# Differential attention run inside and between the tiles of the input projection

## The reference, cut to what matters

```
proj = rms_norm(x, norm_mix_g) @ w_in             # 1024 -> 1952
q_d, k_d, v_d, c_q, c_kv, k_pe = split(proj)      # 512, 512, 512, 256, 128, 32
# differential attention, 8 heads of 2 x 32, values 64 wide, causal, distance bias
a = softmax(q1 k1' * s + bias) - lam * softmax(q2 k2' * s + bias)
o = a @ v;  o = o * rsqrt(mean(o*o) + eps) * out_gain * (1 - lambda_init)
# latent attention, 8 heads
q = rms_norm(c_q)  @ w_uq      # 256 -> 8 x 96, the last 32 of each head rotated
kv = rms_norm(c_kv) @ w_ukv    # 128 -> 8 x (64 key + 64 value)
key = [kv's key, rotated k_pe (shared by the heads)];  o2 = softmax(q key' * s, causal) @ v
x = x + concat(o, rms_norm(o2)) @ w_out           # then memory attention, experts, second block
```

## Time and profile before

| | |
|---|---|
| runs, median (lowest to highest) | 2230.72 us (2230.46 to 2231.52) |
| the profiled execution, its own time | 2235.1 us |
| its span, first to last instruction | 2233.3 us |
| TensorE / VectorE / ScalarE / GpSimd busy | 2000.9 / 1089.9 / 793.4 / 118.6 us |
| mean granted TensorE clock | 0.926 of 2.4 GHz |
| bytes moved by DMA | 261.07 MB, mean 117 GB/s |

### The profile page before, as it was taken

How to read it: one execution, slowest core, us unless ns; L and a number is a source line. 1 busy time by engine, 2 the same in 40 slices (tenths; PEclk the granted TensorE clock), 3 DMA queues, 4 the chain that set the end, 5 groups by cost and what they waited for, 6 DMA issues and landing times.

```text
span 2233.3 us, 25577 instructions
## 1 busy us (share of the span) xinstructions
PE 2000.9 (90%) x9978; PEld 1544.0 (69%) x9978; DVE 1089.9 (49%) x1998; ACT 793.4 (36%) x1655; POOL 118.6 (5%) x85
## 2 busy tenths in 40 slices
PE   7988777897897776999897999999998999999997
PEld 6733444776564445878797888888876768888886
DVE  5565454635321113768555544554465655434444
ACT  4154454444121113653355332222341643322232
POOL 0000000000100003402132000000000000000000
PEclk9966887998899897999998999999998989999999
DMA  5100230334799996121100223233221012322321
GB/s 190 35 0 1 85 97 19 117 114 148 294 411 411 406 393 231 57 67 67 57 1 5 86 95 103 86 95 97 92 95 57 1 44 90 103 95 88 103 94 46
DMA packets 78391, 261.07 MB, mean 117 GB/s; under 512 B 9376, under 2 KB 11680, under 8 KB 77888
## 3 DMA queue, kind: packets, MB, share of 16 engines
q1 hardware_dynamic: 68112, 231.47, 29.1%
q0 software_dynamic: 5040, 19.58, 2.8%
q10 hardware_dynamic: 5120, 8.39, 1.0%
HBM read 242.62 MB, written 16.79 MB: 116 GB/s over the span
## 4 chain that ended last, share of the span: by engine, by line
PE 76%; DVE 10%; DMA 8%; ACT 4%; issue 2%; POOL 0%; ACTq 0%; SPq 0%; DVEq 0%; POOLq 0%
PE ps_pair L276 18%; PE ps_pair L278 17%; PE ps_pair L277 17%; DMA split_acts_as_f<-w_experts 6%; PE ps_pair L794 5%; PE ps_pair L1649 3%; PE ps_turn L807 2%; PE ps_turn L2157 2%; PE ps_out L821 2%; PE ps_shared L821 2%; PE ps_pair L2157 1%; DVE ps_pair L897 1%; PE ps_shared L1660 1%; DMA w_raw<-w_gdnin 1%; PE ps_shared L496 1%
## 5 line engine op out<-in xcount | busy, mean ns | idle before, releaser
L276 PE MATMUL ps_pair<-split_acts,w_high 128*128 128x512 f32 (+1 forms) x1824 | 718.5, 394 | 26.8 <-DVE split_acts L572 9.9
L277 PE MATMUL ps_pair<-split_acts,w_high 128*128 128x512 f32 (+1 forms) x1824 | 710.3, 389 | 0.0
L278 PE MATMUL ps_pair<-split_acts,w_low 128*128 128x512 f32 (+1 forms) x1824 | 710.2, 389 | 0.0
L237 DVE TENSOR_TENSOR w_low<-w_raw,w_high 128x1024 fp32r<-128x1024 f32 (+5 forms) x257 | 291.9, 1136 | 283.5 <-ACT w_high L231 281.6
L276 PEld LDWEIGHTS ps_pair<-split_acts,w_high 128*128 128x128 f32 x1824 | 347.0, 190 | 107.5 <-issue 22.9
L278 PEld LDWEIGHTS ps_pair<-split_acts,w_low 128*128 128x128 f32 x1824 | 346.4, 190 | 72.2
L277 PEld LDWEIGHTS ps_pair<-split_acts,w_high 128*128 128x128 f32 x1824 | 347.1, 190 | 68.8 <-issue 0.2
L231 ACT ACTIVATE w_high<-w_raw 128x1024 fp32r<-128x1024 f32 (+5 forms) x257 | 251.0, 978 | 228.4 <-PE ps_pair L278 203.7
L1649 PE MATMUL ps_pair<-split_acts_as_f 128*64 128x256 f32 x512 | 130.1, 412 | 39.6 <-DMA split_acts_as_f<-w_experts 33.4
L1651 PE MATMUL ps_pair<-split_acts_as_f 128*64 128x256 f32 x512 | 130.6, 413 | 0.0
L1649 PEld LDWEIGHTS ps_pair<-split_acts_as_f 128*64 128x64 f32 x512 | 73.5, 149 | 76.2 <-issue 48.1
(11 more groups left out here) (460 smaller groups left out, 2260.7 us busy)
## 6 DMA issues: line engine op xcount, KB each, us to landing
split_acts_as_f<-w_experts SPq DMA_DIRECT2D x192, 512.0 KB, 14.0
w_raw<-w_gu SPq DMA_DIRECT2D x88, 512.0 KB, 3.4
w_raw<-w_down SPq DMA_DIRECT2D x32, 448.0 KB, 3.3
w_raw<-w_gdnin SPq DMA_DIRECT2D x26, 512.0 KB, 3.4
w_raw<-w_out SPq DMA_DIRECT2D x24, 512.0 KB, 3.5
rows_y<-scratch ACTq DMA_DIRECT2D x64, 128.0 KB, 6.2
w_raw<-w_down SPq DMA_DIRECT2D x16, 512.0 KB, 3.4
w_raw<-w_in SPq DMA_DIRECT2D x15, 512.0 KB, 4.3
```

Source lines behind the costliest of these rows:

```text
L237: dve.tensor_tensor(WL[:, t % SPLIT, 0:kt * m], WRAW[:, t % RING, 0:kt * m], WH[:, t % SPLIT, 0:kt * m].bitcast(F32), ALU.subtract).then_i ...
L276: pe.matmul(out, wh[:, k, :], self.high(k), start=(k == 0), stop=False)
L277: pe.matmul(out, wh[:, k, :], self.low(k), start=False, stop=False)
L278: last = pe.matmul(out, wl[:, k, :], self.high(k), start=False, stop=(k == self.kt - 1))
```

## The change

The input projection's tiles come in another order: c_q and c_kv first (tiles 12, 13, 14), then for each pair of heads its query, key and value tile. Differential attention is cut into calls of `gap(n)`, each of which issues on TensorE the scores of group n, the turning of group n-2 and the values of group n-3, on ScalarE the copies of n-2 and n-3 and then the exponentials of n, on VectorE the weights of n-1 and then the extreme of n. It has one bank pair of its own, `pairs[1]`, and one bank for its outputs. Gaps 0 to 21 stand in the middle of and behind each of tiles 5 to 14 and of `kpe`, gaps 22 to 29 behind every second tile of `uq` and `ukv`, 30 to 32 after them, 33 and 34 at the opening of latent attention. The waits between scores, extremes and exponentials are now for each member of a group (in all five kinds of attention a score matmul and an exponential each signal).

The norms of c_q and c_kv stand behind tiles 1 to 4, the angles behind tiles 1 and 4, the distances behind tile 0. Each rotation is a step of its own (`single`), behind tiles of `uq` and `ukv`, as are the turning of each head's values and the copy of the shared key. The head norm, its split and the first three squares of the latent norm stand behind groups of latent attention. The places in memory change to suit. GpSimd's load of the memory tokens waits for `ukv` too, the load of the router for latent attention's end.

```
+IN_ORDER = (12, 13, 14, 0, 4, 8, 1, 5, 9, 2, 6, 10, 3, 7, 11)
...
+            def gap(self, n):
+                here = lambda k: 0 <= k < len(self.groups)
+                if here(n - 2):
+                    self.number(n - 2)
+                def tensor(pe):
+                    if here(n):
+                        if n % PER_PAIR == 0:
+                            self.wait_scores(pe, n // PER_PAIR)
+                        self.pe_scores(pe, n)
+                    if here(n - 2):
+                        self.pe_turn(pe, n - 2)
+                    if here(n - 3):
+                        self.pe_values(pe, n - 3)
+                def scalar(act):
+                    if here(n - 2):
+                        self.act_turn(act, n - 2)
+                    if here(n - 3):
+                        self.act_out(act, n - 3)
+                    if here(n):
+                        self.act_exp(act, n)
+                def vector(dve):
+                    if here(n - 1):
+                        self.dve_probs(dve, n - 1)
+                    if here(n):
+                        self.dve_max(dve, n)
...
             def pe_scores(self, pe, n):
-                if n >= len(self.banks):
-                    need(pe, "att_act", ("exp", m - len(self.banks)))
-                elif m >= 2:
-                    need(pe, "att_act", ("exp", m - 2))
+                before = m - (len(self.banks) if n >= len(self.banks) else 2)
                 for j, (h, i, r) in enumerate(members):
+                    if before >= 0:
+                        need(pe, "att_act", ("exp", before, sizes[before] - 1 if n < len(self.banks) else j | 1 if len(members) > 2 else j))
...
+            def single(self, k):
...
+                def tensor(pe):
+                    self.waits(pe, k)
+                    claim(pe)
+                    done(pe.matmul(ps_m[r, :], self.perm[r, r], x, start=True, stop=True), "rope_pe", (self.name, k))
+                    held.append(("rope_dve", (self.name, "swap", k)))
+                def vector(dve):
...
+                    done(dve.tensor_tensor(SC[r, k % 2, :], ps_m[r, :], self.sin[r, :], ALU.mult), "rope_dve",
+                         (self.name, "swap", k))
+                    done(dve.tensor_tensor(x, x, self.cos[r, :], ALU.mult), "rope_dve", (self.name, "cos", k))
+                    self.join(dve, k)
...
+        diff.banks = pairs[1:]
...
+        beside = defaultdict(list, {0: [early], 1: [n_cq.part(0), n_cq.part(1), angles_m.part(0)],
+                                    2: [n_cq.root(), n_ckv.part(0)], 3: [n_cq.spread(), n_ckv.root()],
+                                    4: [n_ckv.spread(), angles_m.part(1), early_exps]})
+        first = at_in[8]
+        places = [side[j] for j in range(first, 15) for side in (middle, beside)] + [k_middle[0], k_beside[0]]
+        for n, here in enumerate(places):
+            here.append(diff.gap(n))
+            c, off = divmod(n, 6)
+            if c < QT and off == 3:
+                here.append(turn_values(c))
...
+        for j, rope, gap in ((1, 0, 1), (2, 1, 0), (3, 2, 1), (4, 3, 0), (5, 4, 1), (6, 5, 0), (7, None, 1)):
...
+        for j, rope, head, gap in ((0, 6, None, 0), (1, None, 0, 1), (2, 7, 1, 0), (3, None, 2, 1), (4, 8, 3, 0),
+                                   (5, None, 4, 1), (6, None, 5, 0), (7, None, 6, 1)):
...
+        fl += [diff.gap(n), values_and_keys(7)]
...
+        mla.opened = [diff.gap(n + 1)]
...
+        at_group = [[head_norm.square(0)], [head_norm.sum(0), head_norm.square(1)],
+                    [head_norm.sum(1), head_norm.square(2)], [head_norm.sum(2), head_norm.square(3)],
+                    [head_norm.sum(3), n_mo.part(0)], [head_norm.roots()], [head_norm.spread(0)],
+                    [head_norm.spread(1), s_diff.one(0)], [head_norm.spread(2), s_diff.one(1), n_mo.part(1)],
+                    [head_norm.spread(3), s_diff.one(2)], [s_diff.one(3)], [], [n_mo.part(2)], [], []]
+        for k, stages in enumerate(at_group):
+            mla.beside[k + 1] += stages
+        fl += [mla, n_mo.part(3), n_mo.root(), n_mo.spread()]
...
             need(pool, "rope_dve", ("mla_q", MLA_HEADS))
+            wait_products(pool, "ukv")
             done(pool.dma_start(raw1, a["mem_t"]), "ld_mem", by=16)
```

More of the change, by code:

```diff
@@ L716, in __init__ @@
                 self.m0, self.h0, self.o0 = seen_groups["n"], seen_heads["n"], seen_outs["n"]
[L717 to L720, removed]
+                self.u0, self.opened = [0] * len(self.groups), []
+                if not lazy:
+                    for n in range(len(self.groups)):
+                        self.number(n)
+                sizes.extend(len(group[0]) for group in self.groups)
                 seen_groups["n"] += len(self.groups)
@@ L774, in tensor @@
                 self.pe_scores(pe, 1)
+                for stage in self.opened:
+                    stage.tensor(pe)
                 for n in range(len(self.groups)):
@@ L780, in tensor @@
                         self.pe_values(pe, n - 1)
+                    for stage in self.beside.get(n, ()):
+                        stage.tensor(pe)
                 self.pe_values(pe, len(self.groups) - 1)
@@ L833, in scalar @@
                         self.act_out(act, n - 1)
+                    for stage in self.beside.get(n, ()):
+                        stage.scalar(act)
                 self.act_out(act, len(self.groups) - 1)
@@ L878, in vector @@
                     self.dve_probs(dve, n)
+                    for stage in self.beside.get(n, ()):
+                        stage.vector(dve)
             def dve_max(self, dve, n):
@@ new lines, in program, with values_and_keys, scalar @@
+        rope_q = Rope("mla_q", [ROPED[0:96]] + [AF[0:96, 8 + h, :] for h in range(MLA_HEADS)], 96,
+                      const("perm_mla"), cos_m, sin_m, rope_waits)
+        def values_and_keys(h):
+            turn = Transposes(f"mla_v{h}", [
+                ([(keys_at[h][:, i * P:(i + 1) * P], i * P) for i in range(QT)],
+                 (G[:, 12:16, h * 64:(h + 1) * 64],
+                  lambda b: b[:, :].rearrange("p (i c) -> p i c", c=P)[:, :, 64:128]), None)],
+                wait_first=lambda e: (wait_evac(e, BASE["ukv"] + h), need(e, "mla_dve", "kpe")))
+            mla_v.append(turn.t0)
+            def scalar(act):
+                turn.scalar(act)
+                need(act, "rope_dve", ("mla_q", 0))
+                done(act.copy(keys_at[h][64:96], ROPED[64:96]), "mla_act", "keys")
+            return On(tensor=turn.tensor, scalar=scalar)
@@ L1246, in diff_gain @@
+        mla.opened = [diff.gap(n + 1)]
+        for k in range(len(mla.groups)):
+            mla.number(k)
+            mla.beside[k] = []
+        mla.beside[0].append(diff.gap(n + 2))
         def diff_gain(dve, k, s, label):
```

297 lines of the change are left out of this document (196 added, 101 removed).

## The result

| | before | after | forecast |
|---|---|---|---|
| runs, median (lowest to highest) | 2231.12 us (2230.46 to 2232.25) | 2199.36 us (2197.24 to 2205.47) | 2166.0 us |
| the profiled execution, its span | 2233.3 us | 2203.6 us | |
| first matmul of `out` | 373.7 us | 336.45 us | 309.0 us |
| mean granted TensorE clock | 0.926 | 0.933 | |

The change makes the kernel 31.8 us faster, a ratio of 0.9861 (95% interval 0.9848 to 0.9875). The direction is as forecast and the time lies in the wide range (2134 to 2204), not in the forecast's own (2148 to 2184); the gain is half of the 64.7 us that were forecast.

A forecast was written before the change was run, and what follows sets the result against it. Differential attention was taken as TensorE at the lower clock with gaps, inside a serial stretch to 373.70 us. Parts 1 to 4 put `out` at 309.0, 64.7 earlier: 2230.7 - 64.7 = 2166.0 us; own range 2148 to 2184, wide 2134 to 2204.

The forecast's parts named there:

- part 1: Input projection, tiles 0 to 5: gap 1 begins at 74.9 us, not 54.6; +20.3, of which 15.1 TensorE standing still.
- part 2: 21 gaps in tiles 6 to 14 and `kpe`: 9.5 us a tile, `kpe` ends at 172.4 us.
- part 3: `uq`, `ukv`, rotations, values, keys and 8 gaps: 52 us, to 224.4; then gaps 30 to 32: 9 us, to 233.4.
- part 4: Latent attention with the head norm inside: 67.1 us, to 300.5; then 8.5 of remaining norm, `out` starting at 309.0.
- part 5: The rest of the kernel: later loads cost nothing, finer waits and signals 0, between -3 and +4 us.
- The rival of catching orders: Orders of three engines catch everywhere: projection +22, part 3 64 us, part 4 74 us; total 2198; chance 0.19.
- the ring through VectorE and ScalarE: Part 2: scores wait for exponentials, these for extremes; 2.95 us a gap, 9.5 a tile, longer than TensorE's 8.4.
- The rival of the hidden ring: Ring is hidden and TensorE the bound, in parts 1 to 3: 8.4 us a tile, total 2141; chance 0.20.
- the 0.15 us hops: Part 2: a term of 0.15 us for hops within the 2.95 us ring of each gap.
- the third rival: Clock falls in the mixed stretch: 16.8 us a two-gap tile, +77, part 3 +15; total 2258; chance 0.03.

The follow-up runs named there:

- one group later: Changed kernel with each step of head norm, split and latent squares cut by engine, VectorE's part one group after TensorE's, ScalarE's copy after that; 2177.39 us.
- gaps in a row: Changed kernel with gaps 0 to 21 taken out of the input projection's tiles and set in a row behind `kpe`; 2246.42 us.
- both together: Changed kernel with the angles in pieces behind later tiles and the head norm's vector side a group later; 2165.13 us.

## Why the prediction was right or wrong

| step | forecast | measured | miss |
|---|---|---|---|
| part 1: to gap 1 | 74.9 | 78.2 | +3.3 |
| part 2: to the end of `kpe` | 97.5 more, 172.4 | 94.5, 172.7 | -3.0 |
| part 3: `uq`, `ukv` | 52 | 52.6 | +0.6 |
| part 3: gaps 30 to 32 | 9 | 11.9 | +2.9 |
| part 4: latent attention | 67.1 | 95.1 | +28.0 |
| part 4: rest ahead of `out` | 8.5 | 4.1 | -4.4 |
| part 5 | 0 | 5.4 | +5.4 |

**Part 4 is the step that failed:** the 67.1 us of latent attention with the head norm inside took 95.1. The forecast put it as "VectorE's 3.34 us reciprocal and ScalarE's two changes of tables stand in the pipeline, 4 of them not covered", and priced all else at TensorE's own work, 9.7 us (2.7 of two gaps, 7 of the head norm). It summed durations and never followed the three queues through one group, as part 1 had done for the first tiles. A step with a TensorE or ScalarE half and a vector half was put in one place of the list; VectorE comes to its half while the other is still queued behind copies or turnings, and the next group's extreme stands behind it. The experiments divide the 28.0: 20.3 are the order (95.1 to 74.8, one group later). The root, its table loads and the reciprocal cost 6.5 (74.8 to 68.3) and not 4, which is 2.5. The remaining 5.2 fall in two: 2.5 are there without the head norm (58.6 measured with it behind, 56.1 by the sum), and 2.7 are the head norm's steps without the root (68.3 - 58.6 = 9.7, where 7 of TensorE's at full clock were put; the granted clock is 0.93 over that stage). Neither was looked into further.

The rival of catching orders had this mechanism, with a chance of 0.19 and 74 us for this stage. That its total of 2198 us comes within 2 us of the measured time is luck: it spread its surplus over the wrong stages (+22 in the projection, where there was none) and put 7 here, where 28 were.

**Part 1** held in kind: TensorE stood still in all three of the places named, for 2.72, 2.92 and 7.13 us, where 4.7, 3.6 and 6.8 were worked out. The stands were overestimated, and what made gap 1 late all the same is TensorE's own time: 43.82 us busy at a clock of 0.79, where the sum has 39.5. The forecast named this ("a stand at the lower clock behind each wait could add 4") and left it out of its sum. With the angles moved away the same stretch takes 39.23 us of TensorE at 0.92. That the amount of vector work sets gap 1 is shown by the two runs with moved angles: another place inside the stretch moved the stand, taking it out removed it.

```profile
49.93 1.94 PE L519 MATMUL ps_shared<-consts,roots 128*128 128x128 f32 x8 [2.72 <-DVE roots L474]
54.78 1.87 PE L509 MATMUL ps_shared<-consts,h 128*128 128x1 f32 x8 [2.92 <-DVE g L482]
```

**Part 2** came out right for a partly wrong reason. Results of tiles are taken 9.3 us apart on the mean (ten steps from 80.59 to 173.18, of 8.0 to 10.6 us), as forecast (9.5), but not by the ring through VectorE and ScalarE: TensorE is busy for 93.86 of 94.50 us, and once group 1's scores have begun it waits for an exponential only three times, 0.6 us in all. Taking two results of consecutive tiles, and pieces of the chain of waits between them, which holds TensorE alone there:

```profile
108.34 0.69 DVE L678 TENSOR_TENSOR split_acts_as_f<-ps_pair,h 128x512 f32<-128x512 f32 x1 [1.27 <-PE ps_pair L281]
117.33 0.74 DVE L675 SCALAR_TENSOR_TENSOR g<-ps_pair,columns,h 128x512 f32<-128x512 f32 x1
```

```profile
112.48 0.53 PE ps_pair L874 x3
113.01 0.48 PE ps_turn L886 x3
113.49 0.23 PE ps_pair L279
...
116.26 0.63 PE ps_pair L874 x4
116.89 0.59 PE ps_turn L886 x4
117.48 0.44 PE ps_turn L713 x4
```

The chain does pass through VectorE and ScalarE in other tiles (from 85.7 to 94.0 and from 124.6 to 132.1), where TensorE ends up waiting about 0.2 us; so the ring is nearly as long as TensorE's own work and seldom sets the pace. What was mis-sized is the gap on TensorE: (9.3 - 5.44)/2 = 1.9 us and not 1.48. The 1.48 came from a misreading: a mean clock of 0.62 was taken as "the lower level nearly throughout", and all 94.24 us were halved. A mean of 0.62 is 76% of the time at 1.2 GHz and 24% at 2.4. By the trace's clock records 82.0 of the 94.24 us were at the lower level and 12.2 at the full one, which is 53.2 us at the full level and 1.66 a gap. Turning the values adds under 0.1; the rest of the way to 1.9 is not accounted for, and the times of the 0.15 us hops, which no row shows, were not measured either. The rival of the hidden ring had the mechanism right (next to no waits of TensorE) and its 8.4 us a tile wrong. The forecast's clock, full between tiles as in the earlier trace rows, is borne out at 0.97 (0.56 up to 85 us, 1.00 from there on), and with it the case against the third rival; the run with the gaps in a row shows the lower level coming back (a mean of 0.68) as soon as the tiles are gone.

**Part 3** is right within its bounds: VectorE 39.41 of the 39 to 41 summed. Gaps 30 to 32, alone, took 4.0 us each and not 2.95. Those 2.95 are the ring through VectorE and ScalarE without the scores, which with one bank pair can't start before the exponentials; in the run with the gaps in a row, at clock 0.68, sixteen gaps from 144.66 to 215.07 take 4.4 us each. How much of the surplus here is the clock (0.62) was not divided.

**Part 5.** From `out`'s first matmul to the end the profiled executions take 2203.6 - 336.45 = 1867.2 us after and 2233.3 - 373.7 = 1859.6 before. The other kernels' lie between 1855.2 (signals and finer waits alone) and 1863.9 (gaps in a row), 1860.2 both for both together and for one group later. The execution profiled after is 6.1 us above its own median, and its trace shows where a part of the 7.6 us more arose: 300 matmuls from 944 us on took 64.2 us at a clock of 0.95, with one wait of 2.7 us for ScalarE among them (before 979.17), where the same matmuls take 61.2 to 61.3 in each of the ten other traces. So most of the 7.6 us are that execution's and not the change's. Against the medians 37.2 - 31.8 = 5.4 us of what was won ahead of `out` are missing, and in one group later (59.0 and 54.3) and both together (71.5 and 67.0) about 4.6. The execution of before that was profiled was 4.4 above its median, which may be all of it; which stage held that excess stays open.

**The signals.** Together with the finer waits they are a gain of 5.1 us in the kernel before. The Trainium skill (TensorE: Matmul & The Clock Gate, section "The cost: per-tile semaphore tail") has signals of matmuls serialize at 26 ns each, by which this run would have been an estimated 3 us slower; the measurement decides against a net loss in this kernel. Signals and finer waits were not tried apart, so no run here shows what a signal alone costs.

## What to carry to other kernels

When a step that spans several engines is put inside a pipeline of in-order queues, follow each queue through one turn of the pipeline and ask, for every half, whether its partner's half is done by then; issue the late engine's half one turn after the early one's. A half that is only a wait counts too. A sum of durations said 11 us for this insertion (7 on TensorE, 4 of root and tables); the same instructions cost 36.5 in one order and 16.2 in the other. And a mean clock between the two levels is a mixture: divide the busy time by level before scaling it. Fill work belongs where its engine has slack that the bounding engine does not see: the same angles cost 15.9 us in the tiles where VectorE set the pace and 2.7 where TensorE did.

## What the runs showed of the hardware

- Standing still is paid twice. The same 246 matmuls of latent attention with the head norm were busy for 72.01 us at a granted clock of 0.78 and for 62.35 at 0.91; TensorE is idle for 23.2 us in the first stretch and for 10.5 in the second. By the clock records 31.8 and 12.8 us of the busy time were at 1.2 GHz; with those halved both are 56 us. Of the 22.4 us between the two rows (95.20 and 72.80), 9.7 are TensorE's own busy time.
- The same short matmuls at the two levels: eight that multiply values take 4.46 us at 1.2 GHz and 2.31 at 2.4 (121.78 in the changed kernel), four that turn weights 1.05 (152.45 before) and 0.59 (116.89 after).
- A root inside a stretch of exponentials costs two table loads of 1.28 us each (270.67 and 276.48), the second where the exponentials resume. Leaving them out with the 3.34 us reciprocal of 8 rows between them shortened the stage by 6.6 us in one order and by 6.5 in the other, though ScalarE is busy for only 44.46 of 95.20 and 41.57 of 73.40 us.
